# Two-block model on one core: gate projections by seven half-size products, later modulation rows, the rotation split in two, and output stages that open with two jobs

## The reference, cut to what matters

```python
for l in range(2):
    shift, scale, gate = split(silu(c) @ w_ada[l] + b_ada[l], 3)     # "modulation"
    h = rms_norm(x, norm_g[l]) * (1 + scale) + shift
    u, z_s, q, k, v, z_a = split(h @ w_in[l], 6 x 1024 columns)
    y_s = s5_mixer(u, ...) * silu(z_s)          # the state chain: 64 groups of 64 complex states, then a gated product
    q, k = apply_rope(q), apply_rope(k)         # the rotation: t * cos + swapped halves of t * sin
    y_a = diff_attention(q, k, v, ...) * silu(z_a)
    x = x + gate * (concat(y_s, y_a) @ w_out[l])
```

## Time and profile before

| | us |
|---|---|
| median of 3 runs | 4110.71 (4109.92 to 4111.05) |
| the profiled execution | 4109.78 |
| its span | 4107.6 |
| PE busy, of the span | 3971.8 (97%) |
| DVE busy | 2461.8 (60%) |
| ACT busy | 899.9 (22%) |
| POOL busy | 509.4 (12%) |

### The profile page before, as it was taken

One profiled execution on the slowest core, in us unless ns is written; L12 is line 12 of the kernel. 1 busy time (PEld: TensorE's weight loads), 2 busy tenths in 40 slices (PEclk: granted clock), 3 DMA queues, 4 the chain that ended last, 5 costly groups with the idle time before them and its releaser, 6 DMA issues.

```text
span 4107.6 us, 46555 instructions
## 1 busy us (share of the span) xinstructions
PE 3971.8 (97%) x18296; PEld 3058.0 (74%) x18296; DVE 2461.8 (60%) x4446; ACT 899.9 (22%) x1643; POOL 509.4 (12%) x808
## 2 busy tenths in 40 slices
PE   6899999999999999999999999999999999999999
PEld 3565598755877556987558668888888888888888
DVE  5667657766763675677665446464645356766643
ACT  2222212232011322123421222121212123220000
POOL 0233211111121331111110000000000101100000
PEclk8999999999999999999999999999999999999999
DMA  9643334335652433443444342222222334434423
GB/s 331 208 134 118 118 129 129 121 122 161 187 168 66 132 120 104 148 138 113 140 159 131 125 112 62 67 72 67 72 67 65 114 95 137 134 104 139 133 98 108
DMA packets 382952, 508.01 MB, mean 124 GB/s; under 512 B 44828, under 2 KB 296079, under 8 KB 382223
## 3 DMA queue, kind: packets, MB, share of 16 engines
q1 hardware_dynamic: 300544, 344.36, 26.0%
q0 software_dynamic: 38480, 125.86, 9.9%
q10 hardware_dynamic: 43710, 34.83, 2.6%
HBM read 466.71 MB, written 38.27 MB: 123 GB/s over the span
## 4 chain that ended last, share of the span: by engine, by line
PE 81%; DVE 12%; ACT 4%; issue 2%; DMA 2%; ACTq 0%; DVEq 0%; SPq 0%
PE bank L108 79%; ACT tring L116 2%; PE bank L111 2%; DVE tring L129 2%; DVE tring L123 2%; DVE wring L123 1%; DMA side<-in_w_ada 1%; DVE bank L123 1%; DVE dring L123 1%; DVE sring L144 0%; DVE tring L126 0%; DVE region_b L123 0%; DVE dring L126 0%; DVE s_delta L123 0%; DVE s_in L123 0%
## 5 line engine op out<-in xcount | busy, mean ns | idle before, releaser
L108 PE MATMUL bank<-region_b,wring 128*128 128x256 f32 (+1 forms) x4416 | 1198.7, 425 | 6.8 <-ACT region_b L116 3.9
L108 PEld LDWEIGHTS bank<-region_b,wring 128*128 128x128 f32 x4416 | 828.8, 191 | 300.5 <-issue 205.6
L108 PE MATMUL bank<-region_a,wring 128*128 128x256 f32 (+1 forms) x3360 | 930.4, 430 | 7.1 <-DVE wring L123 7.1
L108 PEld LDWEIGHTS bank<-region_a,wring 128*128 128x128 f32 x3360 | 630.4, 191 | 242.3 <-issue 166.9
L123 DVE TENSOR_TENSOR tring<-bank,tring 128x256 f32<-128x256 f32 (+1 forms) x325 | 141.6, 436 | 436.5 <-PE bank L108 432.8
L116 ACT ACTIVATE tring<-bank 32x512 f32<-32x512 f32 (+2 forms) x341 | 177.8, 523 | 986.4 <-PE bank L108 556.9
L123 DVE TENSOR_TENSOR wring<-wring 128x1024 f32<-128x1024 f32 (+1 forms) x309 | 354.0, 1146 | 25.7 <-PE bank L108 14.4
L153 POOL DMA_DIRECT2D side<-in_w_ada x384 | 209.5, 546 | 1288.3 <-DVE tring L129 834.5
L129 DVE SCALAR_TENSOR_TENSOR tring<-side,cact,tring 128x512 f32<-128x512 f32 x360 | 293.1, 814 | 46.7 <-DMA side<-in_w_ada 8.3
L108 PE MATMUL bank<-wring,region_b 128*128 128x128 f32 (+2 forms) x896 | 216.0, 400 | 6.2 <-ACT region_b L116 6.2
L123 DVE TENSOR_TENSOR bank<-bank,tring 128x256 f32<-128x256 f32 (+1 forms) x309 | 159.8, 517 | 98.4 <-PE bank L108 94.6
(11 more groups left out here) (317 smaller groups left out, 4762.6 us busy)
## 6 DMA issues: line engine op xcount, KB each, us to landing
wring<-in_w_in SPq DMA_DIRECT2D x178, 1024.0 KB, 5.3
side<-in_w_ada POOLq DMA_DIRECT2D x384, 256.0 KB, 3.1
wring<-in_w_out SPq DMA_DIRECT2D x48, 1024.0 KB, 7.7
yaT<-in_w_ada SPq DMA_DIRECT2D x16, 1024.0 KB, 9.2
wring<-in_w_glu SPq DMA_DIRECT2D x16, 1024.0 KB, 7.5
tring<-x_saved SPq DMA_DIRECT2D x48, 256.0 KB, 3.0
gring<-in_w_ada POOLq DMA_DIRECT2D x43, 256.0 KB, 3.1
SS<-in_w_ada SPq DMA_DIRECT2D x8, 1024.0 KB, 9.6
```

Of the source, the lines that this page charges most:

```text
L108: return self.e.matmul(*a, **k) if self.e else self
```

## The change

1. In the state stage the eight gate jobs of each layer become fast jobs. So h is split earlier: `quarter_sums` stand in the last quarter of u's second half, `quarter_rest` and `quarter_last` right after u's transposes, in the first gate job, in pieces of four instead of two. The rates go from 73/79 and 77/79 to 65/79 and 69/79, since a fast job has seven steps and a dense one eight.
2. No modulation rows in the state stage (1.35 becomes 0.0); 2.4 instead of 2.0 in attention, 2.6 instead of 2.1 in the output stage. By the steps' list 0, 127 and 65 rows fall to the stages of layer 0, and the same to those of layer 1.
3. The rotation: DVE multiplies by the cosine first, from the bank; ACT copies after that and releases the bank; the product with the sine and POOL's sum (`rotate_end`) come two steps of the next job later.
4. The output stages of block one take products 1 and 2 of their first two jobs before product 4 of the first; there are two places for `w_sum` 3 there.

```diff
@@ -334,7 +334,7 @@
...
-                lay[0]["s3"] = Room([sb("s3_out0", [P, HT, P], before_states)])
+                lay[0]["s3"] = Room([sb(f"s3_out0{i}", [P, HT, P], before_states) for i in range(2)])
@@ -832,7 +832,7 @@
...
-                               lambda: passed("u", l), lambda: passed("states", l))
+                               lambda: passed("u", l), lambda: passed("u", l))
@@ -851,25 +851,26 @@
...
         def beside_states(l):
             open_split(l)
-            yield from dense(u_job(l, 512))
+            for n, _ in enumerate(dense(u_job(l, 512))):
+                if n == 12:
+                    for k in range(0, HT, 4):
+                        quarter(h_split[l], k, 4)
+                yield
             for h0 in range(0, HT, 2):
                 for n, _ in enumerate(gate_products(l, h0, "za", 5 * HALF)):
-                    if h0 == 0 and n == 3:
+                    if h0 == 0 and n == 1:
                         turn_u(l, 512)
                         do("pe_fence", "u", l)
+                        for name in ("quarter_rest", "quarter_last"):
+                            for k in range(0, HT, 4):
+                                do(name, h_split[l], k, 4)
                     yield
             for h0 in range(0, HT, 2):
-                quarter(h_split[l], h0, 2)
-                do("quarter_rest", h_split[l], h0, 2)
                 yield from gate_products(l, h0, "zs", HALF)
         def gate_products(l, h0, name, n0):
-            job = layer_dense(l, d["w_in"][l], n0 + h0 * P, "save_z", h0, name)
-            for j in range(2):
-                temps.take(name, l, h0 + j)
-            yield from dense(job)
-            for j in range(2):
-                temps.give(name, l, h0 + j)
+            yield from fast(split_job(l, n0 + h0 * P, "save_z", h0, name, s3=states_s3[l]),
+                            before=lambda j: temps.take(name, l, h0 + j), done=lambda j: temps.give(name, l, h0 + j))
@@ -981,10 +982,13 @@
...
-                def done(j):
+                def after(j, which=which):
+                    yield
+                    yield
+                    do("rotate_end", l, h0, which, j)
                     for name in ("rx", "ry"):
                         temps.give(name, l, h0, which, j)
-                yield from fast(split_job(l, (2 + which) * HALF + h0 * P, "rotate", h0, which, s3=lay[l]["s3_in"]), before=before, done=done)
+                yield from fast(split_job(l, (2 + which) * HALF + h0 * P, "rotate", h0, which, s3=lay[l]["s3_in"]), after, before=before)
@@ -1081,7 +1085,8 @@
...
         def add_gated(l, w, rhs, ready, parts=None, s3=None, late=()):
-            for n0 in range(0, D, 256):
+
+            def column(n0, late):
...
                 if parts:
-                    yield from fast(Dense(w, KT, n0, 256, False, rhs, ready, "residual", (l, n0 // P), parts, s3), after, () if n0 else late)
+                    yield from fast(Dense(w, KT, n0, 256, False, rhs, ready, "residual", (l, n0 // P), parts, s3), after, late)
                 else:
                     yield from dense(Dense(w, KT, n0, 256, False, rhs, ready, "residual", (l, n0 // P)), after)
...
+            columns = [column(n0, () if n0 else late) for n0 in range(0, D, 256)]
+            if l < 2:
+                for one in columns[0:2]:
+                    for n in range(2):
+                        next(one)
+                        yield
+            for one in columns:
+                yield from one
...
         def block_one(l):
             beside = beside_states(l)
-            carried[0] = 1.35
+            carried[0] = 0.0
@@ -1127,18 +1141,15 @@
...
-            interleave(state_space(l), beside, [73, 77][l] / 79)
+            interleave(state_space(l), beside, [65, 69][l] / 79)
             do("fence", "ssm", l)
-            do("pe_fence", "states", l)
-            for k in range(0, HT, 2):
-                do("quarter_last", h_split[l], k, 2)
-            carried[0] = 2.0
+            carried[0] = 2.4
...
             interleave(attention(l), beside_attention(l), 40 / 37, 32, 1.5)
             do("fence", "att", l)
             finish_behind(3 - 2 * l)
-            carried[0] = 2.1
+            carried[0] = 2.6
@@ -2425,12 +2436,14 @@
             def rotate(jid, j, l, h0, which):
                 bank = banks.at(jid, j)
-                x, y = temps.at("rx", l, h0, which, j), temps.at("ry", l, h0, which, j)
                 dve.wait_ge(*att_d.of("rope"))
+                dve.wait_ge(*full(jid, j))
+                room(temps.clear("rx", l, h0, which, j))
+                dve.tensor_tensor(temps.at("rx", l, h0, which, j), bank[:, :], cosT[:, :], M).then_inc(*att_d.up("cosine", l, h0, which, j))
+
+            def rotate_end(l, h0, which, j):
+                y = temps.at("ry", l, h0, which, j)
                 dve.wait_ge(*att_a.of("swapped", l, h0, which, j))
-                room(temps.clear("rx", l, h0, which, j))
-                dve.tensor_tensor(x, bank[:, :], cosT[:, :], M).then_inc(*d_step.up())
-                banks.leave((jid, j), dve.mine())
                 dve.tensor_tensor(y, y, sinT[:, :], M).then_inc(*taken_d.up("qk", l, h0, which, j))
@@ -3136,11 +3149,12 @@
             def rotate(jid, j, l, h0, which):
                 bank, y = banks.at(jid, j), temps.at("ry", l, h0, which, j)
                 room(temps.clear("ry", l, h0, which, j))
-                act.wait_ge(*full(jid, j))
+                act.wait_ge(*att_d.of("cosine", l, h0, which, j))
                 for s in range(4):
                     a, z = 32 * s, 32 * (s ^ 1)
                     act.activation(y[z:z + 32, :], bank[a:a + 32, :], ACT.Copy).then_inc(
                         *(att_a.up("swapped", l, h0, which, j) if s == 3 else a_step.up()))
+                banks.leave((jid, j), act.mine())
@@ -3384,7 +3398,7 @@
...
-            def rotate(jid, j, l, h0, which):
+            def rotate_end(l, h0, which, j):
                 dst, b = lay[l]["k" if which else "q"], (h0 // 2) % 2
                 room(passed("ssm", l))
```

More of the change, by code:

```diff
@@ L359, in build @@
                 outT = sb("outT", [P, 4, HT, 256], wide)
-                m["outT"], m["s3"] = [outT[:, i, :, :] for i in range(4)], Room([sb("s3_out", [P, HT, P], wide)])
+                m["outT"], m["s3"] = [outT[:, i, :, :] for i in range(4)], Room([sb(f"s3_out{i}", [P, HT, P], wide) for i in range(2)])
                 wide.close()
@@ L2820, in vector @@
                          angle_turn=angle_turn, rotate_in=rotate_in, scan=scan, rotate_out=rotate_out, lags=lags,
-                         y_turn=y_turn, rotate=rotate, keep_v=keep_v, soften=soften, weigh=weigh, values=values,
+                         y_turn=y_turn, rotate=rotate, rotate_end=rotate_end, keep_v=keep_v, soften=soften, weigh=weigh, values=values,
                          head_out=head_out, glu_gate=glu_gate, glu_out=glu_out, residual=residual,
@@ L3437, in band_fetch @@
                         *band_in.landing())
-            steps = dict(vec_fetch=vec_fetch, ada_fetch=ada_fetch, powers=powers, angles=angles, bc_place=bc_place, lags=lags, rotate=rotate, band=band_,
+            steps = dict(vec_fetch=vec_fetch, ada_fetch=ada_fetch, powers=powers, angles=angles, bc_place=bc_place, lags=lags, rotate_end=rotate_end, band=band_,
                          d_qd=d_qd, oa_store=oa_store, oa_fetch=oa_fetch, v_fetch=v_fetch, band_fetch=band_fetch, fence=fence_of(pool))
```

## The result

The changed kernel takes 4139.77 us (median of 4 runs, 4137.9 to 4140.4), the kernel before 4110.32 us beside it: a ratio of 1.0073, 95% interval 1.0059 to 1.0087. It is 29.5 us slower; 40.1 us faster was forecast, and the range ended at 4100.

What follows compares the result with a forecast made beforehand. It took PE's work plus PE's idle time as the bound: -53.1 + 39.5 (state stages) - 24 + 4 (attention) - 6.5 (openings) = -40.1 us, giving 4070.6 us, with a range of 4040 to 4100.

Steps and rivals of the forecast that it cites:

- gate jobs, PE's work: State stages: seven half-size products replace each dense job, 3.32 us less a job, 53.1 us less PE work in all.
- rotation: Attention: with the cosine first, PE's idle time and clock loss come back, 24 us out of 0 to 42.
- rows in attention: Attention: more modulation rows raise DVE from 65% to 69%, POOL follows; 4 us slower (0 to 15).
- rows in the output stages: Output stages: more rows bring DVE to 79% with no new wait; counted as nothing, up to 10 us.
- openings: Start of the output stages: products of a second job fill PE's waits; gains of 4 us and 2.5 us.
- Gate jobs: the new waits: State stages: PE waits for late folds, 16.3 and 14.2 us, plus 9 us of clock; 39.5 us in all.
- the round it worked out: State stage, layer 0: from y_turn's copy DVE needs 13.5 us to fold 0, so product 7 waits about 3.3 us.
- It keeps up on average: State stages: DVE's load goes from 71% to about 84%, still enough for the fast gate jobs' added work.
- DVE at 80 to 85%: Sign expected in the profile after: DVE's busy share in the state stages if the forecast holds.
- The sign that was named for a time above the forecast: State stages: PE idle over 40 us a layer, or waits released by ACT's Em, would make the forecast wrong upwards.
- the rival of ACT's queue: State stages: save_z waits for folds and delays Em's copies and drive, 112 us of waits; 4143 us, chance 0.10.
- The contention with POOL: Rival, state stages: each of 64 weight sums meets a POOL operation, 46 us more on DVE; 4093 us, chance 0.13.

Runs made afterwards that it cites:

- power_early: The changed kernel with c_power of the next round moved from behind rotate_out to just behind drive, same work; 4083.95 us, ratio 0.9933.
- rot_open: The kernel before with the rotation in two steps and the two-job openings, gates and rows as before; 4059.94 us, ratio 0.9875.
- rows_alone: The kernel before with only the modulation rows' rates changed, to 0, 2.4 and 2.6; 4139.91 us, ratio 1.0068.

## Why the prediction was wrong

| term | forecast | measured |
|---|---|---|
| gate jobs, PE's work | -53.1 | -53.1 less what the clock took; a product is 3.45 us in `power_early` too |
| new waits and clock, state stages | +39.5 | +71 idle, about 28 clock |
| rotation | -24 | -40.8 |
| rows in attention | +4 | +11.2 alone, +10.3 in the changed kernel |
| rows in the output stages | 0 | +19.5 |
| openings | -6.5 | -3.4; -7.7 in `rot_open`, with fewer rows |

The measured column adds up to 31.5 us of loss, and to 29.3 with the 2.2 us of modulation transposes that left the state stages; 29.5 was measured.

**The step that failed** is "Gate jobs: the new waits". Its mechanism was right, and so was the round it worked out. It forecast 30.5 us of waits in two layers, all of them for folds, and there are 71: 25.5 for folds, 20.8 for weight sums, 20.5 released by ACT and 4.4 behind the sums of h's quarters. So the total of the folds was close, though not its parts, and the other 46 us had no term. In detail:

- The waits were read for `fold` 0 alone, one round "against another by hand". `w_sum` 2, which product 6 needs, is behind parts of the same run on DVE in five rounds: 3.2, 3.5 and 3.5 us in layer 0 and 5.28 twice in layer 1. The list of steps gives that order before any run, and one release was followed where a fast job has six.
- In the first two gate jobs of layer 0 `angle_turn` too stands ahead of the fold: 6.35 and 6.28 us where 3.7 and 3.8 were forecast. In later rounds and in layer 1 the folds were less late than forecast (7.9 us instead of 14.2 there).
- ACT was looked at for `save_z` and the copies of Em behind it, and not for the new copy `set_by` and the old one of `turn_u`, which stand behind `sine`, which waits for DVE: 9.34 and 7.77 us, most of it DVE's lateness passed on. `save_z` did cost 3.35 us, but at `lags`, by the bank that it holds, and not by way of Em.
- "The sums of h's quarters cost the same as before" says nothing of their place: in one piece they hold up a product by 0.95 us and `lags`, and PE behind it, by 3.5.
- The clock was given 9 us. The work in the state stages came out 12.2 and 15.0 us shorter instead of 26.5 each, and about 1 us more each for the modulation transposes that left, so that about 28 us went to the lower clock, 0.4 us for each us of idle time.

"It keeps up on average" stood in the text as a comfort, and "DVE at 80 to 85%" as a sign. DVE is at 71% of the longer stage: an engine with room left can be late at each thing that is waited for. The sign that was named for a time above the forecast, over 40 us of idle time a layer, was not reached either: 36 and 37 us of idle time were enough, with the clock's loss on top.

**The rotation.** The mechanism was right and its size too small by 17 us. Idle time fell by 26 of 33 us. The clock term was capped at 9 us from a mean of 0.99 over 983 us. That 0.99 is a rounded figure, and with 0.986 the same sum gives 13 to 14 us; PE's busy time fell by about 14 (7.1 in layer 0, by the two rows above).

**The rows.** "With no wait beyond the opening before; I count nothing for it" was the other failed step. It judged a load of 79% by its mean, as in the state stage. And "POOL has three places and issues ahead, so it follows" did not hold at the higher rates: DVE waits 25.9 us for the rows' transfers in output stage 1 of `rows_alone`, and the late folds stand directly behind such waits.

**The openings** had the right mechanism in layer 0 (6.32 us at the transpose where about 5 was forecast, a gain of 2.5 us where 4 was) and gave next to nothing in layer 1, where 2.8 us of waits were turned into one of 3.08 for `fold` 0 behind the quarter sums and three rows.

**The rivals.** The time is 3 us from the rival of ACT's queue, but not by its mechanism: that was copies of Em held up by `save_z`, and no wait in the state stages of the changed kernel is released by Em. So that the time is near it is chance. The contention with POOL fell in the form it had: the 24 weight sums from 230 to 524 us take 1.30 us on the mean and not 1.95,

```profile
L123 DVE TENSOR_TENSOR wring<-wring 128x1024 f32<-128x1024 f32 x24 | 31.2, 1298 | 5.9 <-PE bank L108 5.1
```

but it holds for `c_power`, which meets POOL's `angles` in 12 of the 14 rounds, at 1.21 against 0.49 us for one operation. The mistake was to spread the price over all sums instead of asking which operation stands there. The Trainium skill, GPSIMD Engine Reference, section Key points, says that GpSimd shares its SBUF interfaces with VectorE and that operations with two SBUF inputs contend. The trace agrees where the two engines run at once, by these 0.72 us.

## What to carry to other kernels

When work of an engine that was never waited for becomes work that products wait for, list every release of the new form (here four sums, a copy and a fold per job, on two engines) and place each behind what is queued ahead of it in every round; the engine's share of busy time bounds the cost from below only. Before giving up such a change, look for an operation in the run ahead that can stand elsewhere: moving one of 4 to 5 us was worth 56 us here, though that did not make the part pay. Count the clock with each wait, here 0.4 us in the state stages and 0.5 in attention for a us of idle time. Ask of every piece of work that waits for a transfer what is queued behind it. And time the parts of a bundled change one by one, since here one part's 43 us were hidden behind another's loss of 70.

## What the runs showed of the hardware

In the two state stages of the changed kernel, with 13 waits of 3.2 to 9.3 us in 683 us, the granted clock is 0.94 and 0.95, where it was 0.99 with almost no waits; in `power_early`, with 12.1 us of waits in 298, it is 0.99, and with 22.1 in 329 it is 0.96. DVE's operation on 320 columns takes 0.49 us alone and 1.21 us beside POOL's `angles`, so that the same six operations of `c_power` take 3.1 us at one place of the round and 5.2 at another. A modulation row of 256 KB lands 3.3 us after its issue (median of 62 in output stage 1 of `rows_alone`, and 3.3 of 20 in the kernel before), so with three places in `side` a faster run of rows makes DVE stand for them.
